# Who computes the low halves of seven weight tiles, and where six selection rounds stand

## What is computed

```
proj = h @ w_in                        # 2184 columns: q, k, v, qi, ki, wi
q = rope(rmsnorm(q));  k = rope(rmsnorm(k));  qi = rope(qi);  ki = rope(layernorm(ki))
topk = 128                             # for each of 512 queries
def block(qb, qib, wib, start):        # 4 blocks of 128 queries
    score = einsum('qhs,qh->qs', relu(qib @ ki), wib)      # 8 index heads
    score = where(causal, score, -inf)
    sel = top_k(score, topk)           # 128 keys for each query
    logits = where(selected and causal, qb @ k * scale, -1e30)
    return softmax(logits) @ v         # 16 heads, 4 key heads
x = x + g1 * (o @ w_out)
```

## Time and profile before

| | |
|---|---|
| median of 3 runs | 1711.98 us |
| profiled execution, its own time | 1711.4 us |
| its span | 1709.6 us |
| PE busy | 1678.5 us (98%) |
| DVE busy | 1019.0 us (60%) |
| ACT busy | 699.3 us (41%) |
| POOL busy | 76.8 us (4%) |

### The profile page before, as it was taken

How to read it: one execution, slowest core, us unless ns; L and a number is a source line. 1 busy time by engine, 2 the same in 40 slices (tenths; PEclk the granted TensorE clock), 3 DMA queues, 4 the chain that set the end, 5 groups by cost and what they waited for, 6 DMA issues and landing times.

```text
span 1709.6 us, 23305 instructions
## 1 busy us (share of the span) xinstructions
PE 1678.5 (98%) x7891; PEld 1338.4 (78%) x7891; DVE 1019.0 (60%) x2010; ACT 699.3 (41%) x1323; POOL 76.8 (4%) x62
## 2 busy tenths in 40 slices
PE   9999999999999998899999999999999999999999
PEld 7788777778877776567888888887888788888887
DVE  7579776667667788846655653466444633333334
ACT  5365676653343336744333323234223433322322
POOL 0020000000000173100000000000000000000000
PEclk9999999999999999999999999999999999999999
DMA  6132444445531120011655553452333233332233
GB/s 257 62 110 81 171 148 148 148 146 203 189 121 50 54 83 26 1 42 58 221 196 189 182 207 99 135 172 87 98 99 99 75 98 99 99 99 88 97 100 110
DMA packets 56777, 202.84 MB, mean 119 GB/s; under 512 B 6577, under 2 KB 6705, under 8 KB 56561
## 3 DMA queue, kind: packets, MB, share of 16 engines
q1 hardware_dynamic: 56688, 201.68, 35.9%
HBM read 198.38 MB, written 2.10 MB: 117 GB/s over the span
## 4 chain that ended last, share of the span: by engine, by line
PE 89%; DVE 6%; ACT 2%; issue 1%; DMA 1%; SPq 0%; DVEq 0%; ACTq 0%
PE bank L485 26%; PE bank L487 25%; PE bank L486 25%; PE bank L671 2%; PE bank L612 1%; PE bank L650 1%; PE bank L528 1%; PE bank L529 1%; DVE WORK L2008 1%; DVE SM L2007 1%; DVE SB L2091 1%; DVE W_lo L1481 1%; PE bank L531 1%; PE bank L534 1%; PE bank L543 1%
## 5 line engine op out<-in xcount | busy, mean ns | idle before, releaser
L485 PE MATMUL bank<-H_hi,W_hi 128*128 128x512 f32 x1336 | 533.6, 399 | 2.0 <-DVE W_lo L1481 1.0
L486 PE MATMUL bank<-H_lo,W_hi 128*128 128x512 f32 x1336 | 520.5, 390 | 0.0
L487 PE MATMUL bank<-H_hi,W_lo 128*128 128x512 f32 x1336 | 520.5, 390 | 0.0
L1481 DVE TENSOR_TENSOR W_lo<-RAW,W_hi 128x512 fp32r<-128x512 f32 x538 | 353.5, 696 | 173.9 <-ACT W_hi L966 157.5
L966 ACT ACTIVATE W_hi<-RAW 128x512 fp32r<-128x512 f32 x538 | 317.2, 625 | 265.5 <-PE bank L487 236.2
L485 PEld LDWEIGHTS bank<-H_hi,W_hi 128*128 128x128 f32 x1336 | 250.8, 188 | 71.3 <-issue 16.8
L486 PEld LDWEIGHTS bank<-H_lo,W_hi 128*128 128x128 f32 x1336 | 250.9, 188 | 54.8 <-issue 4.8
L487 PEld LDWEIGHTS bank<-H_hi,W_lo 128*128 128x128 f32 x1336 | 250.8, 188 | 53.0
L485 PE MATMUL bank<-A_hi,W_hi 128*128 128x512 f32 x352 | 136.9, 389 | 0.0
L486 PE MATMUL bank<-A_lo,W_hi 128*128 128x512 f32 x352 | 136.9, 389 | 0.0
L487 PE MATMUL bank<-A_hi,W_lo 128*128 128x512 f32 x352 | 136.9, 389 | 0.0
(11 more groups left out here) (272 smaller groups left out, 2061.1 us busy)
## 6 DMA issues: line engine op xcount, KB each, us to landing
RAW<-weights SPq DMA_DIRECT2D x269, 512.0 KB, 3.7
AW<-ada SPq DMA_DIRECT2D x100, 512.0 KB, 3.7
X<-x_t SPq DMA_DIRECT2D x4, 512.0 KB, 5.9
y_t<-X SPq DMA_DIRECT2D x8, 256.0 KB, 2.0
LW<-lru_w SPq DMA_DIRECT2D x1, 1024.0 KB, 12.6
QX<-QR SPq DMA_DIRECT2D x40, 16.0 KB
CROW<-crow SPq DMA_DIRECT2D x1, 512.0 KB, 10.7
ROPE<-rope SPq DMA_DIRECT2D x1, 512.0 KB, 13.4
```

The lines of the kernel that those rows point to most:

```text
L485: pe.matmul(dst, wh, ch(hi, k), start=(k == 0), stop=False)
L486: pe.matmul(dst, wh, ch(lo, k), start=False, stop=False)
L487: mm = pe.matmul(dst, wl, ch(hi, k), start=False, stop=(k == chunks - 1))
L1481: dve.tensor_tensor(W_lo[:, w], RAW[:, c:c + HALF], W_hi[:, w], ALU.subtract).then_inc(lo_done, 1)
```

## The change

Fourteen pieces of W_lo (seven tiles: 8, 9, 10, 14, 15, 16 and 17) are written by GpSimd instead of DVE, with the same subtraction. Tiles 11, 12 and 13 stay with DVE. Since `lo_done` is a count in the order of the tiles, each engine waits for the other's pieces where the work passes from one to the other: three waits are added on DVE and POOL for that, and one ahead of attention two. On POOL tile 8 stands between the second and the third power, tiles 9 and 10 behind the third, and tiles 14 to 17 each ahead of the cosine product of i = 10 to 13, behind all index sums.

The selection rounds: three more stand ahead of tile 11's split (10, where 7 were), three more in the query loop (27, where 24 were), and six fewer in attention two (11, one for each of steps 16 to 26, where 17 were: one each in steps 16 to 20, two each in 21 to 26).

```
@@ gpsimd @@
+            def low_weights(tile, halves=range(2)):
+                for half in halves:
+                    sl = (2 * tile.slot + half) % 4
+                    pool.wait_ge(hi_done, tile.n * 2 + (half + 1))
+                    c = tile.slot * TILE + half * HALF
+                    w = slice(sl * HALF, (sl + 1) * HALF)
+                    pool.tensor_tensor(W_lo[:, w], RAW[:, c:c + HALF], W_hi[:, w], ALU.subtract).then_inc(lo_done, 1)
+
             power(0)
             power(1)
+            pool.wait_ge(lo_done, (T_QKV2 + 8) * 2)
+            low_weights(Tile(T_QKV2 + 8))
             power(2)
+            low_weights(Tile(T_QKV2 + 9))
+            low_weights(Tile(T_QKV2 + 10))
             pool.wait_ge(kd_done, 2)
             for i in range(6, 14):
+                if i == 10:
+                    pool.wait_ge(lo_done, (T_QKV2 + 14) * 2)
+                if i >= 10:
+                    low_weights(Tile(T_QKV2 + i + 4))
                 if i in (11, 13):
                     power(3 if i == 11 else 4)
                 if i >= 10:
@@ vector @@
-            split_lo(Tile(T_QKV2 + 8), (0,))
...
-            split_lo(Tile(T_QKV2 + 8), (1,))
...
-            select(2)
+            select(3)
             index_sum(8)
-            split_lo(Tile(T_QKV2 + 9), (0,))
...
-            select(1)
-            split_lo(Tile(T_QKV2 + 9), (1,))
-            select(1)
+            select(2)
             keys_normed(1)
-            split_lo(Tile(T_QKV2 + 10))
-            select(3)
+            select(5)
+            dve.wait_ge(lo_done, (T_QKV2 + 11) * 2)
             for c in range(10, 17):
-                split_lo(Tile(T_QKV2 + c + 1))
+                if c < 13:
+                    split_lo(Tile(T_QKV2 + c + 1))
...
+            dve.wait_ge(lo_done, (T_AO2 + 1) * 2)
             for h in range(4):
                 score(16, h)
...
-ROUNDS_Q = [4, 5, 4, 4, 4, 3]
-ROUNDS_S = [1, 1, 1, 1, 1, 2, 2, 2, 2, 2, 2]
+ROUNDS_Q = [4, 5, 4, 5, 5, 4]
+ROUNDS_S = [1] * 11
```

## The result

The changed kernel takes 1715.59 us (median of 15 runs, 1714.23 to 1716.83), the kernel before 1711.72 us (15 runs, 1710.24 to 1713.55). The ratio is 1.002, interval 1.0013 to 1.0027: slower by 3.9 us. The forecast was 1713.0, with 1708.0 to 1716.5 for 8 in 10. The profiled execution took 1715.86 us, its span is 1714.0.

What follows compares the result with a forecast made beforehand. The prediction took DVE's chain to bound the time up to attention two's first `score`, with PE mostly setting the pace afterwards. 0.1 + 3.0 - 2.0 = +1.1 us gave 1713 us, range 1708.0 to 1716.5 for 8 in 10.

Steps and rivals of the forecast that it cites:

- rival (b): After 631 us GpSimd blocks DVE's rotations and BIAS for 5.1 us in place of 1.0: 1717.2 us, chance 0.19.
- Part 1, up to tile 10: Before tile 11, spared and added DVE work ends in an existing wait; about nothing, taken as 0.1 us.
- The bound of 0.7: Upper bound on the early cost at tile 8's first piece, with DVE holding GpSimd back by one instruction.
- Part 2, the work: Query loop: rounds +5.86 us and block 2's BIAS pair +1.0, less 4.84 of splits; +2.0 us on DVE.
- Part 2, blocking by GpSimd: Query loop after 631 us: GpSimd's subtractions slow five DVE instructions by 0.2 us each, 1.0 in all.
- The upper bound of 1.27 for each: Query loop: most that each of five DVE instructions could lose to a GpSimd subtraction, 6.3 us in all.
- come later against POOL's list: Query loop: block 1's BIAS and tile 13's split shift in time against GpSimd's instructions; no separate size given.
- Part 3: PE waits 1.5 us at tile 14 for GpSimd's W_lo, only there, at no added cost since DVE is later.
- Part 4: Attention two: fewer rounds give back 2.0 us, 0.45 from steps 21 to 25 and 1.5 from step 26.
- The sign that the prediction gave for this credit: The stretch from attention two's first `score` to the output projection was to be 2 us shorter.
- The later of two delays counts: At attention two's first `score`, PE's 1.5 us delay hides behind DVE's 3.0, so only 3.0 counts.
- Rival (a): DVE sets steps 21 to 26, so moved rounds come back in full, 7.5 us: 1707.6 us, chance 0.17.

Runs made afterwards that it cites:

- e2: Kernel before with only the selection rounds moved as in the changed kernel, every W_lo piece staying on DVE: 1719.58 us against 1711.46, ratio 1.0046.
- e6: Changed kernel with GpSimd's eight subtractions for tiles 14 to 17 over 32 columns in place of 512: 1713.68 us against 1711.61 before, ratio 1.0012.
- e1: Kernel before with only the fourteen W_lo pieces moved to GpSimd, all rounds where they were: 1712.90 us against 1711.46, ratio 1.0004.
- e4: Changed kernel with tile 14's two W_lo pieces back on DVE: 1717.76 us against 1711.46 for the kernel before, ratio 1.0035.
- e3: Changed kernel with 26 dummy matmuls filling three PE waits around the start of attention two: 1712.62 us against 1711.46 before, ratio 1.0007.
- e5: Kernel before with 19 dummy matmuls on PE at the start of attention two: 1710.97 us against 1711.61, ratio 0.9994.

## Why the prediction was right or wrong

The forecast's sign, +1.1 us, was right and its size was not. The measured 1715.59 lies inside the range for 8 in 10, but only by the half of rival (b) that the range took in: the forecast's own terms allowed -1.9 to +3.5, and the medians give +3.9, the traces +4.47 (4.46 by the two profiled executions' own times). At a ratio of 1.002 it stands on the edge between "within 0.2%" and "slower". Part of this is luck, since the largest missing term, the clock, was in neither the sum nor a rival. This is the sum, and what stands against each term:

- **Part 1, up to tile 10: 0.1.** GpSimd wrote tile 8's first piece at 568.92 in 1.26 us, and PE began the values 0.2 us earlier than before. Measured 0; right. The bound of 0.7 beside it (DVE holding GpSimd back by one instruction) was the author's estimate; no run shows it at this place, and the slowest of the fourteen pieces took 1.62 us, 0.36 more than that first one.
- **Part 2, the work: 2.0.** Six, sixteen and five rounds stand in the loop, as worked out. Their times and the splits' give 2.0; right. e2 agrees that such work reaches the first `score` in full.
- **Part 2, blocking by GpSimd: 1.0.** The first `score` came 3.8 late, so this term is 1.8. e6 shows 0.98 of it as the new subtractions' doing. The prediction had priced five rotations and BIAS instructions at 0.2 each; it was one that paid, 0.98 in L2028, which reads a single tensor and which the prediction's evidence (two inputs) did not cover. The upper bound of 1.27 for each, on which rival (b) stands, was the author's estimate: no run shows one of the five held for a whole subtraction, and the 0.98 is the most that one of them paid. The other 0.8 comes from instructions that were on GpSimd all along: DVE's list was shifted against them, so tile 13's pair lost 1.1, the rotations' line 0.2, and block 1's BIAS gained 0.5. e2 shows the first and the third with no new instruction on GpSimd, and e1 shows neither with all fourteen. The prediction had named this ("come later against POOL's list") and put no price on it. It also misread a row: when GpSimd's addition ended at 604.58, the rotation of 603.43 had 0.55 us left, not 0.69; no term hangs on that.
- **Part 3: a wait of 1.5 at tile 14, absorbed.** Measured 1.72, and no other for W_lo in the changed kernel. e4 shows that it cost nothing as time there, e1 that it costs 1.25 where DVE is not late. Right in both halves.
- **Part 4: credit 2.0.** From step 18 to the output projection 79.26 us before, 77.15 after: 2.11. Right, and in the steps named: 0.44 up to step 26 and 1.67 in it (0.4 of that because the second BIAS instruction met less of GpSimd there, 0.43 us in place of 0.84, which the prediction did not have). Steps 16 and 17, taken at 0, gave back 0.4 to 0.5 more once the clock is equal (e3 against e5: +3.84 at the first `score`, +3.36 at step 18). The sign that the prediction gave for this credit failed all the same: the stretch from the first `score` to the output projection was to be 2 us shorter and is 0.7 longer (93.07 before, 93.74 after), because the clock's loss lies inside it.
- **What the sum lacked: the clock, 3.2 us.** At step 18 e3 is 3.90 ahead of the changed kernel, e5 0.68 ahead of the kernel before: 3.2 between them. By medians it is less, about 2.1 (2.7 for the changed kernel, 0.6 for the kernel before), with intervals that hold both. The step that failed is "It costs nothing on top ... The later of two delays counts: 3.0". PE's waiting was absorbed as time and then had a price of its own, on which the sum has no term: it waited 1.39 + 1.01 us ahead of attention two, and ran at 0.50 for 13.7 us where it was 3.4 before.

So 3.8 - 0.4 + 3.2 - 2.1 = 4.5, all from traces.

Rival (b) named the right mechanism for the slower side and the wrong share: 1.8 us of blocking, not the 5.1 it needed. Rival (a) is refuted: the steps shrank by 2.1 us, not 7.5, and DVE idled ahead of `score` in steps 21 to 25 for 1.0 to 1.9 us (DVE after, steps 22 and 25):

```profile
695.39 0.56 DVE L2103 CUSTOM_DVE_ANT_0 SB<-bank,BIAS 128x384 f32<-128x384 f32 x1 [1.43 <-issue]
...
712.58 0.56 DVE L2103 CUSTOM_DVE_ANT_0 SB<-bank,BIAS 128x384 f32<-128x384 f32 x1 [1.86 <-issue]
```

## What to carry to other kernels

When a delay on one engine makes PE wait, do not take the wait as free because something else is later (here waits of 1.39 and 1.01 us were followed by 13.7 us at 0.50, where 3.4 were before, and the clock cost 3.2 us): look at the granted clock behind it, in the kernel before too and in more than one run, and price the stretch from matmul rows at both clocks (two rotations took 1.12 us at 1.00 and 2.07 at 0.50). A few dummy matmuls in such waits were worth about 3 us in the changed kernel and did not delay the first `score`; in the kernel before their gain was not resolved. Of six moves of work off a busy engine one carried 1.7 of 2.1 us: find the step after which another engine waits, and move only that one. Work shifted on DVE meets GpSimd's instructions at new places, so its price moves even where GpSimd's list stayed the same (tile 13's pair of splits took 1.29 us before and 2.38 in e2).

## What the runs showed of the hardware that was not expected

- TensorE's granted clock fell to 0.50 behind several waits with matmuls between them, none of them longer than 1.4 us: 1.39 and 1.01 us in the changed kernel, 0.77, 0.56 and 1.05 in the kernel before. In the changed kernel filling either of the two put the fall off by 5 to 6 us, from 658.0 to 663.4 or 664.3, and shortened it, from 13.7 us to 6.8 or 3.4; filling both, and the next, removed it (1.00 from 654 to 674 us in e3).
- One wait of 1.71 us at the same place was followed by a fall in one execution and not in another, of different kernels. Runs of one kernel differ too: mean granted clocks from 0.993 to 0.997, and 3.2 us between the averages of its high-clock and its low-clock runs.
- A single-input DVE `TENSOR_SCALAR` over 128 x 384 took 1.34 us beside a GpSimd subtraction, and 0.36 us without it; over 128 x 512 in step 26 it took 0.84 before, beside a GpSimd subtraction of 128 x 256 that took 1.22 where it takes 0.73 elsewhere, and 0.43 after.
- Two DVE subtractions of 128 x 512 took 1.29 or 2.38 us, with GpSimd's list the same, as their start moved against that list (before and e2).
